# The last token block's MLP with seven products of quarter matrices in place of eight

## What is computed

```
u = rmsnorm(h) ;  proj = u @ w_in
h = h + [A(u) | B(u) | C(u)] @ w_out          # attention, SSD mixer, dilated attention
u2 = rmsnorm(h)
h = h + square(relu(u2 @ w_up)) @ w_down      # w_up 1024x4096, w_down 4096x1024
```

## Time and profile before

| | |
|---|---|
| median of 3 runs | 2590.69 us |
| profiled execution, first to last instruction (the only time the profile gives for it) | 2593.0 us |
| TensorE busy | 2439.2 us, 94% |
| VectorE, ScalarE, GpSimd busy | 48%, 33%, 11% |
| granted TensorE clock, mean | 0.973 of full |
| DMA | 414 MB, mean 160 GB/s |

### The profile page before, as it was taken

One profiled execution on the slowest core, in us unless ns is written; L12 is line 12 of the kernel. 1 busy time (PEld: TensorE's weight loads), 2 busy tenths in 40 slices (PEclk: granted clock), 3 DMA queues, 4 the chain that ended last, 5 costly groups with the idle time before them and its releaser, 6 DMA issues.

```text
span 2593.0 us, 43197 instructions
## 1 busy us (share of the span) xinstructions
PE 2439.2 (94%) x17509; PEld 1425.9 (55%) x17509; DVE 1232.8 (48%) x2843; ACT 846.8 (33%) x1533; POOL 276.3 (11%) x305
## 2 busy tenths in 40 slices
PE   7899879999998999999889999988999999899999
PEld 4455436455444555444455554435555446688887
DVE  3455455566646767742544554125566521322222
ACT  4443244464435443331433231114332111301210
POOL 0111212011101211000111100011101001000000
PEclk9999998899999999999889999999999999999999
DMA  6544363565584667775334555533444544222222
GB/s 210 179 149 163 126 228 117 193 210 176 178 248 155 216 202 227 250 257 183 110 127 140 163 160 156 170 102 125 154 160 162 169 151 134 78 98 91 98 98 80
DMA packets 327588, 414.44 MB, mean 160 GB/s; under 512 B 62111, under 2 KB 248095, under 8 KB 327136
## 3 DMA queue, kind: packets, MB, share of 16 engines
q1 hardware_dynamic: 327392, 411.69, 48.6%
HBM read 300.00 MB, written 111.62 MB: 159 GB/s over the span
## 4 chain that ended last, share of the span: by engine, by line
PE 74%; DVE 6%; ACT 3%; issue 2%; DMA 1%; SPq 1%; POOL 0%; POOLq 0%; DVEq 0%; ACTq 0%
PE core_dense L2279 64%; PE core_spare L2379 2%; PE core_spare L2393 1%; PE core_spare L2367 1%; PE core_spare L2405 1%; PE core_spare L2528 1%; DVE core_col L1993 1%; DVE core_h L1887 1%; DVE core_p L1919 1%; ACT core_p L1695 1%; PE core_spare L2522 1%; PE core_spare L2508 0%; PE core_spare L2462 0%; DVE core_r L1875 0%; PE core_spare L2509 0%
## 5 line engine op out<-in xcount | busy, mean ns | idle before, releaser
L2279 PE MATMUL core_dense<-core_u,core_ring 128*128 128x512 f16 (+2 forms) x4800 | 878.5, 344 | 30.0 <-DVE core_u L1860 16.5
L2279 PEld LDWEIGHTS core_dense<-core_u,core_ring 128*128 128x128 f16 x4800 | 470.3, 99 | 412.2 <-issue 59.6
L2279 PE MATMUL core_dense<-core_r_hi,core_ring 128*128 128x512 f16 (+2 forms) x2560 | 651.5, 340 | 2.6 <-DVE core_h L1887 2.5
L2279 PE MATMUL core_dense<-core_r_lo,core_ring 128*128 128x512 f16 (+2 forms) x1280 | 435.4, 340 | 0.0
L2279 PEld LDWEIGHTS core_dense<-core_r_hi,core_ring 128*128 128x128 f16 x2560 | 251.0, 98 | 198.7 <-issue 7.5
L2279 PE MATMUL core_dense<-tok_u,core_ring 128*128 128x512 f16 x1152 | 271.9, 393 | 17.0 <-DMA core_ring<-scratch_kept_w 17.0
L1887 DVE SCALAR_TENSOR_TENSOR core_h<-core_dense,core_h 128x512 f32<-128x512 f32 (+2 forms) x160 | 94.3, 590 | 341.7 <-PE core_dense L2279 341.4
L1660 ACT ACTIVATE core_r<-core_dense 128x512 f32<-128x512 f32 (+2 forms) x160 | 82.5, 515 | 530.8 <-PE core_dense L2279 530.8
L1875 DVE TENSOR_TENSOR core_r<-core_r 128x512 f32<-128x512 f32 (+2 forms) x160 | 96.1, 601 | 324.4 <-ACT core_r L1660 324.0
L628 PE MATMUL tok_prod<-tok_w_hi,tok_u 128*128 128x512 f16 (+1 forms) x768 | 199.8, 350 | 0.0
L2279 PEld LDWEIGHTS core_dense<-tok_u,core_ring 128*128 128x128 f16 x1152 | 115.4, 101 | 152.1 <-issue 21.5
(11 more groups left out here) (300 smaller groups left out, 2711.0 us busy)
## 6 DMA issues: line engine op xcount, KB each, us to landing
core_ring<-scratch_kept_w SPq DMA_DIRECT2D x264, 512.0 KB, 4.1
scratch_kept_w<-core_ring SPq DMA_DIRECT2D x72, 512.0 KB, 5.4
core_qkv<-out_tok SPq DMA_DIRECT2D x48, 384.0 KB, 5.6
core_staged<-in_w_up SPq DMA_DIRECT2D x32, 512.0 KB, 4.7
core_staged<-in_w_down SPq DMA_DIRECT2D x32, 512.0 KB, 5.4
out_tok<-tok_tok SPq DMA_DIRECT2D x16, 644.0 KB, 3.0
core_piece<-in_c_kt SPq DMA_DIRECT2D x32, 288.0 KB, 3.8
core_piece<-in_c_v SPq DMA_DIRECT2D x16, 576.0 KB, 4.5
```

The costliest lines, as they stand in the source:

```text
L2279: ins = pe.matmul(bank, w[:, k, part, :], s, start=first and j == 0, stop=last and j == 2, skip_group_check=True)
```

## The change

The last block's up and down products are done by a form of Strassen's method with 7 products and 15 additions (Winograd's). Two neighbouring column tiles of the weights are one group: 16 `up` groups and 16 `down` groups, in the order of `Z`: up 0, then four times up groups (4, 4, 4, 3) followed by 4 down groups. In a group the weights are a 2x2 matrix (two halves of the 8 contraction tiles by two output tiles), and the tokens too (two contraction halves by two token halves of 272). Each of the 7 products is 4 tiles x 3 matmuls of 272 columns, 84 matmuls a group. Banks 0, 2 and 3 take a second product on top of the first, once the first has been read off where that is needed.

What each engine does for group n, in the order that its program has it:

- SP loads the raw float32 weights of group n+2 (`zraw`, 1 MB, two buffers) and then the kept high and low tiles of group n+1 (`zplain`, 512 KB and 256 KB).
- GpSimd makes the four weight sums of group n+2 (`weight_sums`: 4 operations of 512 columns into `zsum`, which has one buffer, so it waits for `zw_lo` of group n+1). If group n is an up group, it then mixes that group's squared results (`mix_halves`: 4 operations of 272 columns on `zq`).
- ScalarE copies product 0 out of bank 0 (up groups), makes the high halves of the mixed results of group n-1 if that was an up group (`z_high`, 7x272 columns), the high halves of the weight sums of group n+1 (`z_weights`, 2048 columns), and copies bank 0 again (up groups).
- VectorE reads the banks after steps 1, 2 and 3, makes the low halves of group n-1's results (`z_low`, 7x272 columns) and of the weight sums of group n+1 (`z_weights`, 2048 columns), reads the banks after steps 5 and 6, and in an up group applies relu and square (816 and 272 columns).
- TensorE waits at the start of group n for `zw_lo` of group n.

The diff's core, in the order GpSimd (the sums and its loop over the units), ScalarE, VectorE, TensorE:

```
+    def weight_sums(n):
...
+        pool.wait_ge(zraw_in[n % 2], 16 * (n // 2 + 1))
+        if n:
+            pool.wait_ge(zw_lo, n)
+        pool.tensor_tensor(zsum[:, S_1, :, :], a21, a22, ALU.add).then_inc(z_summed, 1)
+        pool.tensor_tensor(zsum[:, S_3, :, :], a11, a21, ALU.subtract).then_inc(z_summed, 1)
+        pool.wait_ge(z_summed, 4 * n + 1)
+        pool.tensor_tensor(zsum[:, S_2, :, :], zsum[:, S_1, :, :], a11, ALU.subtract).then_inc(z_summed, 1)
+        pool.wait_ge(z_summed, 4 * n + 3)
+        pool.tensor_tensor(zsum[:, S_4, :, :], a12, zsum[:, S_2, :, :], ALU.subtract).then_inc(z_summed, 1)
...
+        elif kind == "z" and k == ZSTEPS:
+            if b + 2 < NZ:
+                weight_sums(b + 2)
+            if Z[b][0] == "up":
+                pool.wait_ge(z_squared, 2 * Z[b][1] + 2)
+                mix_halves(4 + Z[b][1])
...
+    def z_group(n, first, end):
+        kind, i = Z[n]
+        if first == 0:
+            if kind == "up":
+                z_take(n, i, 0)
+            if n and Z[n - 1][0] == "up":
+                z_high(Z[n - 1][1])
+            if n + 1 < NZ:
+                z_weights(n + 1)
+            if kind == "up":
+                z_take(n, i, 4)
...
+    def z_group(n, steps):
+        for step in steps:
...
+            if step == 3:
+                if n and Z[n - 1][0] == "up" and not (kind == "down" and Z[n - 1] == ("up", i + 3)):
+                    z_low(Z[n - 1][1])
+                if n + 1 < NZ:
+                    z_weights(n + 1)
...
+    def z_group(n, first, end):
+        if first == 0:
+            pe.wait_ge(zplain_in[n % 2], 32 * (n // 2 + 1))
+            pe.wait_ge(zw_lo, n + 1)
+            if n == 0:
+                pe.wait_ge(y_act, KT // 2 * ZB)
+                pe.wait_ge(y_dve, KT // 2 * ZB)
```

```
+        def to_halves(b):
+            yield "zload", 0, 0, 0
+            for i in range(2):
+                yield "down", b, 3 * KT + i, 0
+            yield "zsum", 0, 0, 0
+            for i in range(KT):
+                yield "out", ZB, i, 0
+                if i == 3:
+                    yield "zsplit", 0, 0, 0
+            yield "zsum", 1, 0, 0
+            yield "down", b, 3 * KT + 2, 0
+            yield "sum", ZB, 0, 0
+            for i in range(3, KT):
+                yield "y", b, i - 3, 0
+                yield "down", b, 3 * KT + i, 0
+                yield "znorm", i - 3, 0, 0
+            for i in range(5, KT):
+                yield "y", b, i, 0
```

More of the change, by code:

```diff
@@ L707, in settle, with half_groups @@
     return a
-PIECES = (((0, 512),), ((512, 512),), ((1024, 512),), ((1536, 256), (1792, 288)))
+PIECES = (((0, 512),), ((512, 512),), ((1024, 512),), ((1536, 272), (1808, 272)))
 NB = len(PIECES)
+ZB, ZW = NB - 1, 272
+def half_groups():
+    out = [("up", 0)]
+    for q in range(4):
+        out += [("up", g) for g in range(4 * q + 1, min(4 * q + 5, 16))]
+        out += [("down", m) for m in range(4 * q, 4 * q + 4)]
+    return out
+Z = half_groups()
+NZ = len(Z)
+ZSTEPS = 7
+B11, B22, B21, B_1, B_2, B_3, B_4 = range(7)
+S_1, S_2, S_3, S_4 = range(4)
+ZPRODUCTS = ((0, "a11", B11), (1, S_2, B_2), (2, S_3, B_3), (3, S_1, B_1), (0, "a12", B21), (2, "a22", B_4), (3, S_4, B22))
 BW = 544
@@ L980, in plan @@
             yield "sum", 0, 0, 0
-            for b in range(NB):
+            for b in range(ZB):
                 beside = iter(())
@@ L1022, in plan @@
                     yield "sum", b + 1, 0, 0
+            for n in range(NZ - 1):
+                yield "z", n, 0, ZSTEPS
+            for k, (first, end) in enumerate(((0, 2), (2, 4), (4, ZSTEPS))):
+                yield "z", NZ - 1, first, end
+                yield "y", ZB, 2 * k, 0
+                yield "y", ZB, 2 * k + 1, 0
             yield "tail", NB - 1, 0, 0
-            yield "y", NB - 1, 7, 0
+            yield "y", ZB, 6, 0
+            yield "y", ZB, 7, 0
             yield "tail", NB - 1, 1, 0
@@ L2232, in _ @@
                         out(b, i)
-                    elif kind == "sum":
+                    elif kind == "sum" and b < ZB:
                         norm(b)
@@ new lines, in z_part @@
+                def z_part(n, step, js):
+                    kind, i = Z[n]
+                    bank, which, right = ZPRODUCTS[step]
+                    out_ = z_banks(n)[bank][:, 0:ZW]
+                    for j in js:
+                        if kind == "up":
+                            hi, lo = zu[:, 0, right, j, :], zu[:, 1, right, j, :]
+                        else:
+                            at = (i // 4 * 4 + j) % 5
+                            hi, lo = zr_hi[:, right, at, :], zr_lo[:, right, at, :]
+                        w_s = z_operand(n, which, j)
+                        for k, (part, moving) in enumerate(((0, hi), (0, lo), (1, hi))):
+                            last = pe.matmul(out_, w_s[:, part, :], moving, start=step < 4 and j == 0 and k == 0, stop=j == 3 and k == 2, skip_group_check=True)
+                    if 3 in js:
+                        last.then_inc(z_done, 1)
@@ L2610, in _ @@
                 for kind, b, i, k in units:
+                    if kind == "z":
+                        z_group(b, i, k)
                     if kind == "col":
```

251 lines of the change are left out of this document (241 added, 10 removed).

## The result

The changed kernel takes 2638.93 us in the median of 4 runs (2633.07 to 2643.68), beside 2587.75 for the kernel before on the same chip: 1.0189 times as long, 95% interval 1.017 to 1.0207. That is 51 us slower; forecast were 63, with the range from 2610 to 2688. The profiled execution is the fastest of the four (2633.07); its span, from the first to the last instruction, is 2631.2 us.

A forecast was written before the change was run, and what follows sets the result against it. Before, TensorE's columns bound the last block; after, a ring across engines through single-buffered `zsum` would set up groups. Start 2217.6, groups 419, clock 8 and end 11.5 gave a 2656 us span, so 2654 us median, range 2610 to 2688.

The forecast's parts named there:

- Part 1: Last block's products on TensorE: 2688 matmuls in place of 3072, 9.7 us a group, 44 us less if TensorE alone decides.
- Part 2: Engines feeding the products: a ring of 16.5 us per up group and 9.7 per down group, 419 us for all.
- The collision: VectorE's two squares beside GpSimd's weight sums: 1.55 us on top of the ring per up group, bounds 0 and 2.0.
- The ring without a collision: From one `zw_lo` write to the next around an up group: sums, mixes, `z_high`, `z_low`, `z_weights`, waits and hand-overs, 15.0 us.
- The rule on the port pair: A VectorE operation with two SBUF inputs and a GpSimd operation exclude each other; without it 24 us lower.
- The first rival: No collision on SBUF between VectorE and GpSimd: 15.0 us per up group, 24 us less, 2630; chance 0.24.
- Part 3: TensorE's clock drops in up groups' idle time; slower starts cost 2 us four times, 8 us in all.
- Part 4: Moving `out` and norm among `down` units: the gap goes, 2.4 us idle for `y`, 1.5 for loads; group 0 at 2217.6.
- Part 5: The kernel's end: 2.5 us for the last group's `y` steps and about 9 us for six turns behind, 11.5 together.
- The third: Rival: engines overlap, the ring closes within 9.7 us and TensorE decides, 2537 us; chance 0.06.
- The second: Rival: GpSimd at its fastest row, 1.04 us for 512 columns, 13.5 a ring without collision, 2604 us; chance 0.08.

The follow-up runs named there:

- Experiment 2: The changed kernel with VectorE's two squares of every up group cut to 16 of 272 columns; 2620.19 us, 1.0111 of the kernel before.
- experiment 3: The changed kernel with next weights put ahead of the last up group's hidden values on ScalarE and VectorE; 2604.14 us, 1.0049 of the kernel before.
- experiment 6: The changed kernel with the four weight sums of a group on VectorE in place of GpSimd; 2600.54 us, 1.0033 of the kernel before.
- Experiment 5: The kernel before, eight products kept, with only the last block's out products, norm and squares moved among the third block's last groups; 2580.36 us, ratio 0.9961.
- experiment 8: The kernel of experiment 7 with the weight sums on VectorE in place of GpSimd; 2567.89 us, 0.9908 of the kernel before.
- experiment 9: The kernel of experiment 7 with ScalarE's first-product copy ahead of `z_weights` and VectorE's `z_low` after the group's last add; 2590.24 us, 1.0003 of before.
- experiment 7: The kernel of experiment 3 with squares on ScalarE and its `z_weights` ahead of its first-product copy; 2599.14 us, 1.0029 of the kernel before.

## Why the prediction was right

**Part 1, the products: right as a count, and rightly said to decide nothing.** A down group at TensorE's pace takes 9.73 us where 9.7 were forecast.

**Part 2, what feeds them: the mechanism held link by link, the size was 7% too high.** 15.44 us per up group were measured where 16.5 were forecast. 16 times the difference is 17 us, and that is about the whole miss in this stretch: from group 0's first matmul (2208.49) to the last group's end (2621.54) are 413.1 us, forecast 419 + 8 + 2.5 = 429.5. The size rests on two terms that were too large:
- The collision was put at 1.55 us, all of the squares' time. Experiment 2 gives 1.0. The second sum lasts 2.08 us for 1.28 and the third 1.48: 0.8 and 0.2 us. The squares held GpSimd off for less than their own 1.07 and 0.5 us. The first of them began while GpSimd's first sum still ran (2250.70, against 2251.33), and I read it so that a part of its time passed in that wait; this is argued, not shown.
- The ring without a collision is 14.4 us (experiment 2), not 15.0. The durations were right one by one (sum 1.28 for 1.27, mix 0.76 for 0.76, `z_high` 1.79 for 1.8, `z_low` 2.14 for 2.2, `z_weights` 2.28 for 2.35), but I added them with hand-overs of 0.06 and waits of 0.08. In the trace most operations start 0.04 to 0.1 us ahead of the recorded end of the one that they follow on their engine. Only two of the four waits on GpSimd's own results show, ahead of the fourth sum and the fourth mix (0.07 and 0.08), and the hand-overs between engines are 0.03 to 0.15.

**The rule on the port pair held.** Experiments 2, 3 and 6 show that two operations that read two SBUF operands each, on VectorE and on GpSimd, shut each other out, in both directions. Most of the time of one is added to the other's: 2.69 us for a mix of 0.76 that met a `z_weights` of 2.28. The Trainium skill, page "SBUF — State Buffer", section on SBUF's two separate sides, states this exclusion. The first rival, which went without it, had the time more closely (2630) and even the group (15.0), for the wrong reason: the forecast's ring was 0.6 us too long, and that makes up for over half of the collision.

**Part 3, the clock: the cost to TensorE was about right, but little of it reached the total.** The prediction took 2.5 us at the lower clock from the earlier trace rows. That was misread. The row from 2222 to 2224 has 0.58 in the mean, so the clock was back at 1.00 only about 0.3 us before 2224, some 3.8 us behind the first `up` matmul at 2219.86. In the change, TensorE began the first down group of each of the three first sections at the lower clock. The second of them (columns as in the earlier trace rows):

```profile
2397.34:2401.34 4.00, 4.00 (x18) 2.67 (x19) 1.39 (x4) 0.00 (x0) 3.88 (x4) 0.50 0.01 4
```

Its 84 matmuls took 12.1 us, those of the other two 11.4 and 12.4, so 1.7 to 2.7 us more than the 9.73 of the pace, where 2 were forecast. But the writes of `core_zw` around these groups stand 10.2, 10.9 and 11.2 us apart, only 3.1 us over the pace together. The write for the next group comes over a microsecond before TensorE has finished this one, and the forecast had not counted that slack. Then 5.9 us went to a wait that I had not counted: in the last section no up group stands between the last hidden values and the first `down` product that needs them, so that TensorE waits for `z_low`. The two together are 9.0 us where 8 were forecast, and that is luck.

**Part 4, the move: right in its sum, in part by luck.** No load came late, for no wait of TensorE there names a DMA, and the gap went. The forecast had 2.4 us for late copies of `y` and 1.5 for late loads; the copies cost 1.95 and 2.51 us and the loads nothing. Group 0 started at 2208.5, not 2217.6, but this execution ran some 9 us ahead where the program is still the same. GpSimd at the same place of the program, before and in the change:

```profile
1995.33 2.53 POOL L1544 TENSOR_TENSOR core_grown<-core_xbc,core_grown 128x512 f32<-128x512 f32 x2 [13.52 <-ACT core_grown L1741]
```

```profile
1986.25 2.53 POOL L1654 TENSOR_TENSOR core_grown<-core_xbc,core_grown 128x512 f32<-128x512 f32 x2 [13.51 <-ACT core_grown L1890]
```

From there to group 0 it is 222.2 us; forecast were 2217.6 less 1995.33, 222.3. Experiment 5 gives the worth of the move, 0.39%.

**Part 5, the end: right.** 9.7 us of span lie behind the last group, forecast 9.

**Rivals.** The third, that engines overlap enough to close the ring in 9.7 us, was rightly held small for this order of steps. It took another order on both engines and two moves of work, the squares and the sums (experiment 8), to come near it, and the prediction named none of these. The second fell: GpSimd's sums took 1.28 us, never 1.04.

What stays open: why the trace gives "issue" for most of TensorE's waits for `core_zw`, and how much of experiment 8's remaining 24 us another order, experiment 9's above all, would give back. A second buffer for the weight sums, 8 KB a partition more, would break the ring at the place where it closes; it was not tried.

## What to carry to other kernels

When a change trades TensorE's columns for sums on other engines, follow the single buffers round: add up what must happen between two writes of the same tile, across all engines, and compare that with TensorE's time per group; the sum per engine (here 8.4 us of 9.7) did not show it. On one engine, what the next group needs goes ahead of what is needed later: that exchange alone gave back 35 of 51 us. And count the two-operand work of VectorE and GpSimd as that of one engine. As a bound this sum of single durations is a little too high: it was 13.9 us in experiment 3, where the group took 12.97. Each addition that goes from GpSimd to VectorE takes half as long there, and shortens that common sum even if VectorE gets busier.

## What was not expected of the hardware

VectorE adds 512 columns with two SBUF operands in 0.68 us, GpSimd in 1.28. (The Trainium skill, page "Trainium Architecture — The Big Picture", section on the five engines, has GpSimd at half VectorE's speed for elementwise work; the trace agrees, with 1.9 times the time.) On 16 columns GpSimd takes 0.22 us, so that the other 496 columns cost 1.06 of the 1.28 us.

An operation that is shut out shows no idle time in front: the wait is in its own recorded duration (2.69 us for a mix of 0.76 in experiment 3, 3.05 for a sum of 1.28 in experiment 7, each beside one long VectorE operation). Such a stall is seen only against the same form elsewhere.
